# The squares and roots of two latent norms, moved from the preparation of a sparse attention into the attention itself

## What is computed

```python
h = u @ w_in[l]
q_a, kc, vc, ksl, vsl, kwn, vwn, gate_logits, cq, ckv, k_rope = jnp.split(h, split_at, axis=-1)
o_nsa = nsa_mixer(...)          # sparse attention
o_mla = mla_mixer(cq, ckv, ...) # latent attention

def rms_norm(x, g):
    xf = x.astype(jnp.float32)
    return (xf * lax.rsqrt(jnp.mean(xf * xf, -1, keepdims=True) + EPS) * g).astype(x.dtype)

q = (rms_norm(cq, q_norm_g) @ w_uq)     # cq: 384 columns of each token
kv = (rms_norm(ckv, kv_norm_g) @ w_ukv) # ckv: 256 columns of each token
```

## Time and profile before

| | |
|---|---|
| median of 3 runs | 2171.02 us (2167.63 to 2173.47) |
| the profiled execution, its own time | 2167.02 us |
| its span, first to last instruction | 2165.4 us |
| PE busy | 95% of the span |
| DVE busy | 70% |
| ACT busy | 45% |
| POOL busy | 35% |

### The profile page before, as it was taken

One profiled execution on the slowest core, in us unless ns is written; L12 is line 12 of the kernel. 1 busy time (PEld: TensorE's weight loads), 2 busy tenths in 40 slices (PEclk: granted clock), 3 DMA queues, 4 the chain that ended last, 5 costly groups with the idle time before them and its releaser, 6 DMA issues. The chain is left out here.

```text
span 2165.4 us, 28251 instructions
## 1 busy us (share of the span) xinstructions
PE 2065.4 (95%) x10025; PEld 1721.1 (79%) x10025; DVE 1515.9 (70%) x2342; ACT 984.9 (45%) x1893; POOL 755.2 (35%) x702
## 2 busy tenths in 40 slices
PE   5999999999998999889998899989999999999997
PEld 4888888878887788778787778878888888878885
DVE  6877777768688613679988678765655555558689
ACT  2533333334545221578878467734533333334443
POOL 0366556620200000167555145401145655630201
PEclk9999999999999999999999999999999999999998
DMA  7245544458941422010000000042233233348975
GB/s 276 88 162 170 175 163 158 166 177 254 295 154 34 174 61 72 6 42 1 1 1 1 1 1 1 30 156 81 90 112 107 89 118 106 127 149 259 298 246 97
DMA packets 193632, 254.38 MB, mean 117 GB/s; under 512 B 18192, under 2 KB 116560, under 8 KB 193495
## 3 DMA queue, kind: packets, MB, share of 16 engines
q1 hardware_dynamic: 178088, 208.04, 28.8%
q0 software_dynamic: 15408, 44.57, 7.9%
HBM read 212.72 MB, written 43.52 MB: 118 GB/s over the span
## 5 line engine op out<-in xcount | busy, mean ns | idle before, releaser
L3012 POOL TENSOR_TENSOR nsa_exps<-nsa_exps,nsaa_factor 128x512 f32<-128x512 f32 (+1 forms) x102 | 96.3, 972 | 91.2 <-DVE nsaa_factor L2999 91.2
L767 DVE TENSOR_TENSOR ffn2A_u<-ffn2A_u,ffn_banks 128x512 f32<-128x512 f32 x60 | 41.2, 687 | 118.1 <-PE ffn_banks L711 118.1
L1301 DVE SCALAR_TENSOR_TENSOR late_part_late<-ada_rows,far_silu_c,late_part_late 128x1024 f32<-128x1024 f32 x56 | 108.8, 1942 | 2.0 <-DMA ada_rows<-in_w_ada 2.0
L588 ACT ACTIVATE ffn1A_t_hi<-ffn1A_t 128x512 fp32r<-128x512 f32 x80 | 48.5, 628 | 131.0 <-POOL ffn1A_t L581 94.9
L588 ACT ACTIVATE ffn2A_t_hi<-ffn2A_t 128x512 fp32r<-128x512 f32 x80 | 48.4, 628 | 121.5 <-POOL ffn2A_t L581 91.8
L2077 PE MATMUL in_acc<-mix_in_w_hi,mix_in_u_hi 128*128 128x494 f32 x256 | 99.5, 389 | 1.4 <-PEq L86 0.9
L2077 PE MATMUL in_acc<-mix_in_w_lo,mix_in_u_hi 128*128 128x494 f32 x256 | 99.1, 387 | 0.0
L2077 PE MATMUL in_acc<-mix_in_w_hi,mix_in_u_lo 128*128 128x494 f32 x256 | 99.0, 387 | 0.0
L711 PE MATMUL ffn_banks<-ffn1S_s_hi,ffn1A_t_hi 128*128 128x512 f32 x240 | 93.8, 391 | 0.0
L2949 ACT ACTIVATE nsaa_turned_hi<-nsaa_ring 128x512 fp32r<-128x512 f32 (+1 forms) x148 | 84.7, 602 | 19.3 <-PE nsaa_out_ps L2923 12.2
L711 PE MATMUL ffn_banks<-ffn1S_s_hi,ffn1A_t_lo 128*128 128x512 f32 x240 | 93.4, 389 | 0.0
(11 more groups left out here) (651 smaller groups left out, 6992.2 us busy)
## 6 DMA issues: line engine op xcount, KB each, us to landing
ada_rows<-in_w_ada POOLq DMA_DIRECT2D x56, 512.0 KB, 4.7
ffn_raw_g<-in_ffn_wg SPq DMA_DIRECT2D x44, 512.0 KB, 3.7
ffn_raw_u<-in_ffn_wu SPq DMA_DIRECT2D x44, 512.0 KB, 4.9
early_w<-in_w_ada SPq DMA_DIRECT2D x16, 512.0 KB, 7.2
mix_in_w_raw<-in_w_in SPq DMA_DIRECT2D x32, 247.0 KB, 2.7
ffn_rest<-in_ffn_wd SPq DMA_DIRECT2D x29, 256.0 KB, 5.3
hidden<-ffn1A_c SPq DMA_DIRECT2D x22, 256.0 KB, 4.4
hidden<-ffn1A_u SPq DMA_DIRECT2D x22, 256.0 KB, 5.0
```

The costliest lines, as they stand in the source:

```text
L588: act.activation(self.b_hi[w][:, :], self.block_of(w), ACT.Copy).then_inc(self.rounded, 1)
L767: dve.tensor_tensor(out, base, bank, ALU.add).then_inc(self.mixed, 1)
L1301: dve.scalar_tensor_tensor(out=part_late[:, v, :], in0=ada[:, n % 2, :], scalar=silu_c[:, k:k + 1], in1=part_late[:, v, :], op0=ALU.mult, ...
L3012: pool.tensor_tensor(at, at, by, ALU.mult).then_inc(self.weighed, 1)
```

## The change

A new class, `LatentNorms`, holds the squares, roots and the scaling, and hangs on `beside`, which ACT and DVE now call too:

- ACT: after the exponentials of score steps 0 to 15 one `Square` each; after those of score step 16 the two `Sqrt`.
- DVE: the constant eps is set after the maximum of score step 0; the inverse of the roots is taken after the maximum of score step 18.
- POOL: the scalings follow units 20 to 35 (before: 0 to 15); the first waits until the inverse is known. `pool_price` moves its 1100 ns to the same units. `act_price` and `dve_price` stay as they were.

The preparation loses the 16 squares, the two roots, the inverse and the constant. One unnamed tile (`base`) is put into the memory layout of the latent attention's inputs.

```diff
@@ -2351,18 +2346,6 @@
                 for g in range(GROUPS):
                     rows = h[:, :, col_v[br] + g * HD:col_v[br] + (g + 1) * HD]
                     act.activation(v[:, br, g, :, 0:HD], rows, ACT.Copy).then_inc(v_hi_done, 1)
-            count = 0
-            for n, (col, rank) in enumerate(LATENTS):
-                for i in range(TT):
-                    if count:
-                        act.wait_ge(squared, count)
-                    act.activation(square[:, 0:rank], h[:, i, col:col + rank], ACT.Square,
-                                   accum_out=sums[:, n, i:i + 1]).then_inc(squared, 1)
-                    count += 1
-            act.wait_ge(squared, count)
-            act.wait_ge(eps_set, 1)
-            for n, (col, rank) in enumerate(LATENTS):
-                act.activation(root[:, n, :], sums[:, n, :], ACT.Sqrt, scale=1.0 / rank, bias=eps[:, 0:1]).then_inc(rooted, 1)
             for kv in range(2):
                 act.wait_ge(hid_done, kv + 1)
                 act.activation(hidden[:, kv, :, :], hid_ps[:, kv, :, :], ACT.Gelu).then_inc(gelu_done, 1)
...
@@ -2400,8 +2382,6 @@
                 dve.wait_ge(v_hi_done, n + 1)
                 rows = h[:, :, col_v[br] + g * HD:col_v[br] + (g + 1) * HD]
                 dve.tensor_tensor(v[:, br, g, :, HD:2 * HD], rows, v[:, br, g, :, 0:HD].bitcast(F32), ALU.subtract)
-            dve.wait_ge(rooted, 2)
-            dve.reciprocal(rstd[:, :, :], root[:, :, :])
             dve.wait_ge(c_hi_done, 1)
             dve.tensor_tensor(kc_lo[:, :, :], kc_ps[:, :, :], kc_hi[:, :, :].bitcast(F32), ALU.subtract)
             dve.wait_ge(c_hi_done, 3)
...
@@ -2412,6 +2392,55 @@
             dve.tensor_scalar(gates[:, :, :], gates[:, :, :], 1.0, None, ALU.add)
 
 
+class LatentNorms:
+
+
+    FIRST = 2 * TT + 4
+
+    def __init__(self, nc, s, h, rstd):
+        self.h, self.rstd = h, rstd
+        self.square = s.sb("square", [P, Q_RANK])
+        self.sums = s.sb("square_sums", [P, 2, TT])
+        self.eps = s.sb("latent_eps", [P, 1])
+        self.root = s.sb("latent_root", [P, 2, TT])
+        self.eps_set, self.squared, self.rooted, self.known = (s.sem(x) for x in ("eps_set", "squared", "rooted", "known"))
+
+    def act(self, act, m):
+
+        if m < 2 * TT:
+            n, i = divmod(m, TT)
+            col, rank = LATENTS[n]
+            if m:
+                act.wait_ge(self.squared, m)
+            act.activation(self.square[:, 0:rank], self.h[:, i, col:col + rank], ACT.Square,
+                           accum_out=self.sums[:, n, i:i + 1]).then_inc(self.squared, 1)
+        elif m == 2 * TT:
+            act.wait_ge(self.squared, 2 * TT)
+            act.wait_ge(self.eps_set, 1)
+            for n, (col, rank) in enumerate(LATENTS):
+                act.activation(self.root[:, n, :], self.sums[:, n, :], ACT.Sqrt, scale=1.0 / rank,
+                               bias=self.eps[:, 0:1]).then_inc(self.rooted, 1)
+
+    def dve(self, dve, m):
+
+        if m == 0:
+            dve.memset(self.eps[:, :], EPS).then_inc(self.eps_set, 1)
+        elif m == 2 * TT + 2:
+            dve.wait_ge(self.rooted, 2)
+            dve.reciprocal(self.rstd[:, :, :], self.root[:, :, :]).then_inc(self.known, 1)
+
+    def pool(self, pool, n):
+
+        n -= self.FIRST
+        if 0 <= n < 2 * TT:
+            if n == 0:
+                pool.wait_ge(self.known, 1)
+            which, i = divmod(n, TT)
+            col, rank = LATENTS[which]
+            at = self.h[:, i, col:col + rank]
+            pool.tensor_scalar(at, at, self.rstd[:, which, i:i + 1], None, ALU.mult)
+
+
 class Masks:
 
 
...
@@ -2475,6 +2504,7 @@
         with Scope(nc, stage) as s:
             self.uq_hi = s.sb("uq_hi", [P, self.q_chunks, HEADS * MD], F32R)
             self.uq_lo = s.sb("uq_lo", [P, self.q_chunks, HEADS * MD], F32R)
+            s.sb("base", [P, 448])
             self.rope = RopeLatent(s, "rope_q", HEADS, COL_QM, MD)
 
             def units_of(col, chunks, gain_at, hi, lo):
...
@@ -2700,7 +2730,7 @@
 
     kind, n, k = step
     own = 145 + (4 - u.first_row(u.blocks[k])) * u.keys * 1.67
-    return own + (1100 if u.gate is not None and n < 2 * TT and k == len(u.blocks) - 1 else 0)
+    return own + (1100 if u.gate is not None and 0 <= n - LatentNorms.FIRST < 2 * TT and k == len(u.blocks) - 1 else 0)
 
 
 PRICES = {"pe": pe_price, "act": act_price, "dve": dve_price, "pool": pool_price}
...
@@ -2938,6 +2968,8 @@
                     made = act.activation(u.kept(r, u.room), u.seen(r, self.scores[:, m % 2, :]), ACT.Exp,
                                           bias=self.neg_max[:, n % SUMS, r:r + 1], accum_out=self.sums[:, n % SUMS, r:r + 1])
                 made.then_inc(self.exped, 1)
+                if self.beside is not None:
+                    self.beside.act(act, m)
                 if self.next is not None and m == len(self.score_no) - 1:
                     self.next.over_keys(act)
             elif kind == "turn":
...
@@ -2980,6 +3012,8 @@
                     dve.wait_ge(self.guarded, guards)
                     top = dve.tensor_scalar(at, at, -NO_KEY, None, ALU.min)
                 top.then_inc(self.maxed, 1)
+                if self.beside is not None:
+                    self.beside.dve(dve, m)
             elif kind == "turn":
                 j = self.turn_no[step]
                 cols = slice(u.first_row(u.blocks[k]) * P, HALF)
...
@@ -3011,7 +3045,7 @@
             by = self.factor[:, n % SUMS, top:4].unsqueeze(2).to_broadcast([P, 4 - top, u.keys])
             pool.tensor_tensor(at, at, by, ALU.mult).then_inc(self.weighed, 1)
             if self.beside is not None and k == len(u.blocks) - 1:
-                self.beside(pool, n)
+                self.beside.pool(pool, n)
 
 
 def sparse_attention(nc, stage, h, k_hi, k_lo, v, kc_hi, kc_lo, vc, gates, ident, ident_r, causal, window, compressed,
...
@@ -3074,14 +3108,6 @@
                         g * TT + tiles.index(i), branch == 0, branch == 2, gate, [g * TT + i] if branch == 0 else [], 2, 220,
                         rooms[branch, i, g])
 
-        def scale_latents(pool, n):
-
-            if n < 2 * TT:
-                which, i = divmod(n, TT)
-                col, rank = LATENTS[which]
-                at = h[:, i, col:col + rank]
-                pool.tensor_scalar(at, at, rstd[:, which, i:i + 1], None, ALU.mult)
-
         class Folding:
 
 
...
@@ -3118,7 +3144,7 @@
                     vacant[b].append(rooms[b, i, g])
         units = [unit(g, i, b) for g in range(GROUPS) for i in tiles for b in range(3)]
         return Attend(nc, stage + "a", units, Staging(), Folding(), ident, ident_r, 6,
-                      {"pe": (0, 1, 2), "act": (2, 0, 1), "dve": (2, 1, 0, 3), "pool": (0,)}, 0, ahead=ahead, beside=scale_latents)
+                      {"pe": (0, 1, 2), "act": (2, 0, 1), "dve": (2, 1, 0, 3), "pool": (0,)}, 0, ahead=ahead, beside=LatentNorms(nc, s, h, rstd))
 
 
 def latent_attention(nc, stage, h, k_hi, k_lo, kv_hi, kv_lo, ukv_hi, ukv_lo, v, ident, ident_r, causal, inputs, behind):
```

10 lines of the change are left out of this document (2 added, 8 removed).

## The result

| | kernel before | kernel after |
|---|---|---|
| median of 17 runs each | 2171.02 us (2166.26 to 2177.27) | 2177.76 us (2173.77 to 2181.89) |
| ratio | | 1.0031, 95% interval 1.0023 to 1.0040 |

The changed kernel is slower by 6.7 us. The forecast of 2175.5 us was 2.3 us too low; the time lies in the range of 2168.5 to 2182.5 us.

The account below looks back on a forecast made before the run. In the sparse attention PE and DVE set the pace, ACT having 15% left. The terms 5.6 - 1.0 + 0.2 + 0.4 - 0.65 gave 4.55 us, so 2171.02 + 4.5 = 2175.5 us, range 2168.5 to 2182.5.

Parts of the forecast that it names:

- The planner's other shifts: Sparse attention: order shifts of one to five steps, either sign, given 0 with bounds of 1 us each way.
- Squares and roots: Sparse attention, ACT: 11.2 us of added work between 928.8 and 972 us, of which 5.6 us show.
- The rule of three quarters: Sparse attention: three quarters of ACT's 7.43 us idle time is filled by its new work, so 5.6 us stay.
- The second load: Sparse attention: the 1.28 us table load ahead of the exponential after the roots may fall into a wait for a maximum.
- The buffer: Sparse attention: ACT may fall about one score step behind before PE stands, -1.0 us (bounds 0 and -2).
- The clock: Sparse attention: PE standing more loses some of its full clock, at most a few tenths of a us.
- The preparation, -0.65 us: End of the preparation: PE needn't wait for ACT's Gelu after its multiplications, gain 0.65 us (bounds 0 and 0.67).
- POOL: +0.4 predicted: Sparse attention: scalings behind units 20 to 35 delay weightings after unit 24, net +0.4 us (bounds -0.4 and +1.5).
- POOL was the brake: Rival, sparse attention: taking 17 us off POOL speeds up units 0 to 15, 2166.5 us; chance 0.06.
- ACT's work is exposed whole: Rival, sparse attention: none of ACT's 7.43 us idle time is usable, 11.65 us slower, 2182.7 us; chance 0.25.
- The squares hide: Rival, sparse attention: all ACT idle time is used and the preparation's gain remains, 2171.0 us; chance 0.16.
- The signs: Preparation and attention: first transpose 0.6 to 0.7 us earlier, ACT busy 95% or more, stretch to fourth unit 5 us longer.

Follow-up runs that it names:

- e1: Kernel after with squares, roots, inverse and eps back in the preparation; scalings and planner's price stay late: 2172.04 us, ratio 1.0002.
- e5: Kernel before with only the 16 scalings moved behind units 20 to 35, planner's price and order unchanged: 2169.40 us, ratio 0.9984.
- e4: Kernel after without both square roots and their two table loads; the inverse is taken of the sums: 2175.49 us, ratio 1.0019.
- e2: Kernel after with the scalings priced at units 0 to 15, so PE, ACT and DVE keep the order of before: 2174.96 us, ratio 1.0018.
- e11: Second measurement of the kernel before with only the scalings moved behind units 20 to 35: 2170.87 us, ratio 0.9998.
- e7: Kernel after with the roots behind score step 32 instead of 16 and the inverse after 34: 2179.23 us, ratio 1.0027.
- e3: Kernel after without the 16 squares, row sums set to a constant on DVE, roots kept: 2175.51 us, ratio 1.0019.

## Why the prediction was nearly right, step by step

**Sum of the parts.** By differences of whole attentions: order of the planner 2.14 (e1 less e5), scalings late by themselves -0.38 (e5 less before), squares 2.29 (e4 less e1), roots 3.07 (after less e4); together 7.12. That these add up proves nothing, for each profile but the first and last enters once with either sign; the check on them is the second measurement of the order (2.12, after less e2) and of squares and roots together (5.38, e2 less e5; 5.85 with e11 in place of e5). With the preparation's mean gain of 0.6 us (below) the sum is 6.5, against 6.7 by the medians.

**The forecast's sum failed at one term: "The planner's other shifts ... I give them 0 and bounds of 1 us each way".** They cost 2.1 us, twice measured (2.6 with e11 for e5), outside these bounds. I had seen the shifts in the order and had argued from the price of the scalings, not from what the shifted transposes would meet: the ring. With 2.1 in its place the sum would have been 6.6 us, close to the 6.7 that the chip showed; that it comes so close is luck, since ACT's part was 0.6 too low and POOL's 0.8 too high.

**Squares and roots, as predicted, but not by the way I gave.** Predicted 5.6 of 11.2 us (three quarters of ACT's idle time used), measured 5.36 (e1) and 5.38 (e2 less e5). The rule of three quarters mixed two cases that behave in opposite ways: of the squares, each short and at its own step, two thirds are hidden (and they are 6.5 us of work, not 8.2); of the root block, which is longer than what two score buffers hold, about a tenth is (2.72 us of 3.05 show in B, 2.87 in D of e7). The halves agree by chance. The other 0.55 us of the 3.07 between after and e4 lie in A, ahead of any root, where the granted clock was 0.92 in after and e7 (33.21 and 33.25 us) and 0.94 in e4 (32.66). So they probably belong to the clock and not to the roots; no run shows it for sure.

**The second load "may fall into a wait".** It didn't. ACT is busy for 9.15 of 9.42 us in B. The Trainium skill ("ScalarE: Activation LUTs", "What ACT_TABLE_LOAD costs") gives 1283 ns for a load, and both loads took 1.28 us here too. The drain of about 1380 ns that it adds shows nowhere: the roots start 0.01 us behind the first load, the exponential 0.01 us behind the second, and the measured price of the whole block, 2.7 to 2.9 us, is under its 3.05 busy us.

**The buffer, -1.0 us: it gave nothing that I can find.** C is 0.72 us shorter than before, but 0.51 of this belongs to the planner's order (e1 less e5). Together with DVE's inverse (+0.2) I had 4.8 us for ACT's part and it was 5.4.

**The clock.** I wrote that PE's standing idle costs at most a few tenths of a us by the clock. After and e7 bear that out behind the roots, where their granted clock stayed at 1.00; e3 doesn't: 1.4 us in C behind the roots, and up to 0.7 in A.

**The preparation, -0.65 us.** Right as a mean, and not seen in the profiled pair. PE waits for no Gelu any more, as foretold. PE, ACT's Gelus and PE's next multiplications in after:

```profile
898.84 16.75 PE L2310 MATMUL sparse_in_hid_ps<-sparse_in_blocks,cmp_w_w 128*128 128x128 f32 x128
...
915.42 0.61 PE L2317 MATMUL sparse_in_out_ps<-sparse_in_hidden,sparse_in_w 128*128 128x128 f32 x4
```

```profile
908.48 0.38 ACT L2351 ACTIVATE sparse_in_hidden<-sparse_in_hid_ps 128x256 f32<-128x256 f32 x1 [3.44 <-PE sparse_in_hid_ps L2310]
...
915.62 0.38 ACT L2351 ACTIVATE sparse_in_hidden<-sparse_in_hid_ps 128x256 f32<-128x256 f32 x1 [6.76 <-PE sparse_in_hid_ps L2310]
```

But the multiplications themselves took longer: 16.75 us in after against 15.39 in e2. Most of their time, first in after, then in e2, with a granted clock of 0.85 and 0.93:

```profile
898.76:915.11 16.35, 16.35 (x128) 16.35 (x127) 16.10 (x34) 6.22 (x10) 0.00 (x0) 0.85 0.00 1
```

```profile
901.64:916.80 15.16, 15.16 (x129) 15.16 (x128) 14.91 (x31) 6.78 (x11) 0.00 (x0) 0.93 0.00 1
```

In the four profiles in which ACT holds the end with squares and roots (before, e1, e5, e11), it is 16.62 or 16.63 us from the first of these multiplications to the next matrix's first, whatever the clock; in the other nine it is 15.18 to 16.76, mean 16.01. So the gain is -0.1 to 1.4 us, 0.6 in the mean: ACT's squares, which held the end, had been hiding how long the multiplications took. My bound of 0.67 took the clock of one execution for a constant.

**POOL: +0.4 predicted, about -0.4 measured.** The delay on POOL that I worked out is there, but it doesn't lengthen the attention. POOL behind unit 24 in after, beside the earlier trace rows:

```profile
1060.33 4.03 POOL L3046 TENSOR_TENSOR nsa_exps<-nsa_exps,nsaa_factor 128x512 f32<-128x512 f32 x4 [4.12 <-DVE nsaa_factor L3033]
1064.34 1.25 POOL L2441 TENSOR_SCALAR h_h<-h_h,sparse_rstd 128x384 f32<-128x384 f32 x1
1065.57 4.03 POOL L3046 TENSOR_TENSOR nsa_exps<-nsa_exps,nsaa_factor 128x512 f32<-128x512 f32 x4
1069.58 1.24 POOL L2441 TENSOR_SCALAR h_h<-h_h,sparse_rstd 128x384 f32<-128x384 f32 x1
1070.79 0.61 POOL L3046 TENSOR_TENSOR nsa_exps<-nsa_exps,nsaa_factor 128x256 f32<-128x256 f32 x1
```

Weightings and scalings follow one another with no gap, so unit 26 is indeed late. PE's waits for POOL rose from 0.4 to 1.0 us in after, but both of them (12.9 and 73.3 us behind the attention's first transpose) come before the first scaling, which starts at 127; at the scalings' new place there is none. In e5, with the order of before, there are 2.1 us:

```profile
PE nsaa_ring L2934 <- POOL nsa_exps L3041: 2.1, 3, 0.9
```

Two of the three, 1.15 us, stand 140 us behind the first transpose, where before has its one wait of 0.37: 0.8 us more, inside the 0.9 that I gave. Yet e5's attention isn't longer; that PE would have waited for another engine there is my reading, not shown. The rival "POOL was the brake" falls with e5 and e11: with 17 us taken off POOL, A, B, C and D together changed by +0.33 and -0.07 us (91.10 and 90.70 against 90.77), where the rival needed several us less. The stretch behind unit 15 was 0.6 us shorter in after than before, where growth by over 1.5 would have gone against my reading of POOL.

**The rivals.** "ACT's work is exposed whole" (2182.7) is refuted for the squares and true of the roots. "The squares hide" (2171.0) is refuted by e4 against e1, where 2.3 us of them show, and by the roots. The chance of 0.31 was for slower by over 0.3%; measured are 0.31%, with an interval of 0.23 to 0.40%, so that this line isn't clearly passed, and a third of the loss came by a cause that stood in no rival. The chance also rested on a slip: 8.7 + 0.2 + 0.4 - 0.65 is 8.65, not 6.5. The first rival passes 6.5 us from 6.55 us exposed on, when over a third of ACT's idle time stays unfilled, and not only from 8.7.

**The signs.** Two loads of 1.28 us stand about the roots, and PE goes on at once behind its multiplications in the preparation, as foretold. Others came out weaker: over A and B of after ACT is busy for 39.35 of 42.63 us, 92% and not 95%; in the profiled pair the attention's first transpose is no earlier against the preparation's start (32.0 us before, 32.1 after); and from the first exponential to the fourth unit's last weighting it is 26.8 us in after and 24.3 before, 2.5 us more and not 5. That stretch ends ahead of the roots, so it could hold the squares' loss only.
